# Decoder trunk with a mixture of experts: expert weights take the units of their ring in the order in which these are released

## The chip, the cores and the metric

The kernel runs on one core of a Trainium2 chip. The metric is the device time of one execution in microseconds (us). The kernel before took 1750.72 us, the median of three runs (1747.68, 1750.72 and 1752.5).

## What is computed

A trunk of two layers over 512 tokens of width 1024, all in float32. Layer 0 mixes tokens by RWKV-7 and by sparse attention, layer 1 by stick-breaking attention. Each layer then has a mixture of experts, which is all that the change touches:

```python
# hierarchical_moe: top-1 of 4 groups, then top-2 of its 8 experts; 32 experts in all
expert_idx, gates = ...                    # two experts for each of the 512 tokens
def expert_block(args):                    # w1, w3: 1024 x 512, w2: 512 x 1024
    xb, e = args
    return (jax.nn.silu(xb @ w1[e]) * (xb @ w3[e])) @ w2[e]
y = jnp.sum(y_asg.reshape(n_tok, 2, d) * gates[..., None], axis=1)
x = x + y
```

After both layers comes a final RMSNorm.

## The kernel before

A layer's end has two stages, each closed by a barrier of all engines. `router` does the mixer's output projection, chooses the experts and scatters the tokens' rows, sorted by expert, to the DRAM tensor `sorted_rows`: POOL issues two indirect DMAs for each of four tiles of 128 tokens (L581). `experts` then goes through the 32 experts, 48 rows each.

**Weights.** Each expert has three pieces (part 0 is w1, part 1 is w3, part 2 is w2) of 2 MiB each, 16 KB on each of 128 partitions. They are read from HBM once, into a ring of 11 units in SBUF. Piece p (expert p // 3, part p % 3) lies in unit p % 11 (`place`), so it may be loaded only once piece p - 11 has been used. SP issues all these loads (L634, and L641 for halves) and the loads of rows (L1055), in one written order, and waits in that same order.

The first eight units are loaded at the start of `router`. Units 8 and 9 (`GUEST`) first hold the output projection's weights. Once this is done, SP issues unit 8, then waits for the scatter of the rows, loads the rows of experts 0 to 2 from `sorted_rows` into three slots (`SLOTS`), and issues unit 9. Unit 10 is loaded at the start of `experts`. From there, for each expert n from 3, SP waits until the rows of expert n - 3 have been transposed, loads the rows of expert n, and then each part of expert n after the wait of `freed`: on `up_done` if the unit held w1 or w3, on `down_done` if it held w2. The last two experts (`HALVED`) come in halves, so that the first half of a product can start on the first half of the weights.

**TensorE's order in `experts`.** `turn_rows` transposes an expert's rows (L714), `gain_rows` on DVE copies them out with a gain (L783). `up` multiplies them by w1 and w3 (L726, L727; the two products lie side by side in the array, in eight steps over k); ACT takes the silu of one (L839), DVE multiplies it by the other (`hidden`, L791). `up` of expert n waits for `xT_out` (the rows of n) and for `hid_done` (the `hidden` of n - 1, which frees the PSUM bank). `turn_hidden` transposes the result (L748), `down` multiplies by w2 (L756), and `spread` (L778) puts the rows back on the tokens, added by DVE (L823). Below expert 19 (`OWN`) TensorE does `up` of n, `turn_hidden` of n - 1 and `down` of n - 1; from there on it does `up`, `turn_hidden` and `down` of the same expert.

At the layer's end the units of `GUEST` take what comes next: three tiles of the second layer's q/k/v weights (`LoadedAhead`, L1213) or the final norm's gain (`GainAhead`, L1228).

Of the kernel before, what the change touches and what calls it, by code (L numbers as in the profile page):

```python
# [31 lines left out]
KD = D // P  # L32
# [5 lines left out]
N_EXP = 32  # L38
# [13 lines left out]
class Core:  # L52


    def __init__(self, nc, ctx):
        self.nc, self.ctx, self.made, self.of_stage = nc, ctx, 0, []
# [118 lines left out]
class Arriving(InPlace):  # L175
# [6 lines left out]
    def load(self, sp):  # L182
        for t in range(TT):
            sp.dma_start(self.x[:, t, :], self.x_dram[t * P:(t + 1) * P, :]).then_inc(self.x_in[t], 16)
# [107 lines left out]
def router(nc, c, ctx, ps, x, xn, yT, gain_dram, w_group, w_expert, xrows, r, wts):  # L292
# [8 lines left out]
    LAST = TT - 1  # L301
    tok = lambda i: slice(order[i] * P, (order[i] + 1) * P)
    wr = c.sb("w_router", [P, KD, NL], ctx=ctx)
    g = r.gain
# [46 lines left out]
    with nc.Block() as block:  # L351

        @block.sync
        def _(sp):
            sp.dma_start(g[:, :], gain_dram.rearrange("(p k) -> p k", k=KD)).then_inc(gain_in, 16)
            sp.dma_start(wr[:, :, 0:N_GRP], w_group.rearrange("(p k) n -> p k n", k=KD)).then_inc(w_in, 16)
            for i in range(N_GRP):
                lo = N_GRP + i * EPG
                sp.dma_start(wr[:, :, lo:lo + EPG],
                             w_expert[i].rearrange("(p k) n -> p k n", k=KD)).then_inc(w_in, 16)  # L360
            wts.load(sp, range(GUEST[0]))
            sp.wait_ge(out_done, 2 * TT)
            wts.load(sp, GUEST[:1])
            for j in range(2):
                sp.wait_ge(scattered[j], 16 * TT)
            for n in range(SLOTS):
                r.load_rows(sp, xrows, n, n * CAP)
            wts.load(sp, GUEST[1:])

        @block.tensor  # L370
        def _(pe):
# [216 lines left out]
SLOTS = 3  # L588
XG = MB * D // (P * P)
UNIT, UNITS = KD * FF, 11  # L590
PARTS = (KD, KD, KF)
GUEST = (8, 9)
EXTRA = (0, 1, 2)


def place(n, part):

    use, j = divmod(len(PARTS) * n + part, UNITS)
    return j, use


HALVED = (N_EXP - 2, N_EXP - 1)
LOADS = [sum(place(n, part)[0] == j for n in range(N_EXP) for part in range(len(PARTS))) for j in range(UNITS)]


class ExpertWeights:
# [4 lines left out]
    def __init__(self, c):  # L611
        self.c = c
        self.landed = [c.lasting_sem(f"unit_in{j}") for j in range(UNITS)]
        self.rest_landed = [[c.lasting_sem(f"rest_in{n}_{part}") for part in range(2)] for n in HALVED]

    def start_layer(self, w1, w3, w2):
        self.dram, self.unit = (w1, w3, w2), {}
# [19 lines left out]
    def load_half(self, eng, n, part, half):  # L637

        k = PARTS[part] // 2
        rows = slice(half * k, (half + 1) * k)  # L640
        eng.dma_start(self.view(n, part)[:, rows, :], expert(self.dram[part], n, 2 * k)[:, rows, :]).then_inc(  # L641
            self.rest_landed[HALVED.index(n)][part] if half else self.landed[place(n, part)[0]], 16)

    def arrived(self, pe, n, part):

        j, use = place(n, part)
        pe.wait_ge(self.landed[j], 16 * (use + 1))

    def load_guest(self, eng, w_dram):

# [8 lines left out]

    def end_layer(self, c):  # L660

        c.of_stage += self.landed + [s for pair in self.rest_landed for s in pair]
        self.__init__(c)


def expert(w, e, k):

    return w[bass.ds(e, 1)].rearrange("o (p k) n -> p (o k) n", k=k)
# [3 lines left out]
def experts(nc, c, ctx, ps, x, xrows, r, gain_dram, wts, ahead):  # L672
# [8 lines left out]
    x_rows, g, row_of, slot_row, slot0, rows_in = r.x_rows, r.gain, r.row_of, r.slot_row, r.slot0, r.rows_in  # L681
# [11 lines left out]
    half = (slice(0, MB), slice(UP, UP + MB))  # L693
    GROUPS = 2 * TT

    xT_done, xT_out = c.sem("xT_done"), c.sem("xT_out")
    up_done, silu_done, hid_done = c.sem("up_done"), c.sem("silu_done"), c.sem("hid_done")
    hidT_done, hidT_out = c.sem("hidT_done"), c.sem("hidT_out")
    down_done, high_out, low_out = c.sem("down_done"), c.sem("y_high_out"), c.sem("y_low_out")
    compared, sel_made, spread_out, added = c.sem("compared"), c.sem("sel_made"), c.sem("y_spread"), c.sem("x_added")  # L700
    far_out, own = c.sem("further_slot_out"), c.sem("dve_own")

    LAST, OWN = N_EXP - 1, 19
    XSLOT, XUSES = N_EXP % SLOTS, N_EXP // SLOTS
    slot = lambda n: n % SLOTS
    use = lambda n: n // SLOTS
# [3 lines left out]
    def turn_rows(pe, j, u):  # L710
        pe.wait_ge(rows_in[j], 16 * u + 16)
        nc.tensor.ldweights(c.half[:, :], tile_position=(0, 0))
        for i in range(XG):
            last = nc.tensor.transpose(ps_x[:, i:XG * P:XG], x_rows[j][:, i, :], c.ident[:, :])  # L714
        last.then_inc(xT_done, 1)

    def up(pe, n, b, w1, w3, first_half, second_half):
        pe.wait_ge(xT_out, n + 1)
        if not isinstance(n, int) or n >= 1:
            pe.wait_ge(hid_done, n)  # L720
        for k in range(KD):
            if k == 0:
                first_half()
            if k == KD // 2:
                second_half()
            nc.tensor.matmul(ps_1[0:MB, :], xT[b][:, k, :], w1[:, k, :], start=k == 0, stop=k == KD - 1)  # L726
            last = nc.tensor.matmul(ps_3[UP:UP + MB, :], xT[b][:, k, :], w3[:, k, :],  # L727
                                    start=k == 0, stop=k == KD - 1)
        last.then_inc(up_done, 1)

    def up_expert(pe, n, before):
        def first_half():
            for part in range(2):
                wts.arrived(pe, n, part)

        def second_half():
            if n in HALVED:
                for part in range(2):
                    pe.wait_ge(wts.rest_landed[HALVED.index(n)][part], 16)

        up(pe, n, n % 2, wts.view(n, 0), wts.view(n, 1), first_half, second_half)
        spread(pe, before, range(TT // 2))
# [119 lines left out]
    with nc.Block() as block:  # L862

        @block.sync
        def _(sp):
            wts.load(sp, range(GUEST[-1] + 1, UNITS))

            def freed(n, part):

                gone, was = divmod(len(PARTS) * n + part - UNITS, len(PARTS))  # L870
                sp.wait_ge(down_done if was == 2 else up_done, gone + 1)

            for n in range(SLOTS, N_EXP):
                sp.wait_ge(xT_done, n - SLOTS + 1)
                r.load_rows(sp, xrows, slot(n), n * CAP)
                if n in HALVED:
                    for part in (0, 1):
                        freed(n, part)
                    for half_ in range(2):
                        for part in (0, 1):  # L880
                            wts.load_half(sp, n, part, half_)
                    freed(n, 2)
                    wts.load(sp, [len(PARTS) * n + 2])
                else:
                    for part in range(len(PARTS)):
                        if len(PARTS) * n + part >= UNITS:
                            freed(n, part)
                            wts.load(sp, [len(PARTS) * n + part])
            if ahead is not None:
                users = [max(n for n in range(N_EXP) for part in range(len(PARTS)) if place(n, part)[0] == j) for j in GUEST]  # L890
                sp.wait_ge(down_done, max(users) + 1)
                ahead.load(sp, [wts.unit[j] for j in GUEST])

            def more(e, b, m):
                end = sp.value_load(r.x_end[0:1, bass.ds(e, 1)], min_val=MB, max_val=N_ROWS)
                row = nc.s_assert_within(sp.snap(end - b * MB), 0, N_ROWS - MB, skip_runtime_bounds_check_because="further blocks lie inside the expert's rows")
                sp.wait_ge(down_done, m + N_EXP)
                r.load_rows(sp, xrows, XSLOT, row)
                for part in range(len(PARTS)):
                    wts.load_whole(sp, e, part, EXTRA[part])  # L900

            further(sp, more)

        @block.tensor
        def _(pe):
            turn_rows(pe, 0, 0)
            up_expert(pe, 0, -1)
            turn_rows(pe, 1, 0)
            for n in range(1, OWN):
                up_expert(pe, n, n - 2)  # L910
                turn_hidden(pe, n - 1)
# [15 lines left out]
            def more(e, b, m):  # L927
                n, u = m + N_EXP, m + XUSES

                def landed(part):  # L930
                    pe.wait_ge(wts.landed[EXTRA[part]], 16 * m + 16 * (LOADS[EXTRA[part]] + 1))

# [261 lines left out]
def odd_columns(g):  # L1194

    lo = (g * GC + 2 * D) % (3 * D)
    return slice(lo, lo + GC)


class LoadedAhead:  # L1200
# [5 lines left out]
        self.c, self.w = c, w_dram.rearrange("(p k) n -> p k n", k=KD)  # L1206
        self.raw_in = [c.lasting_sem(f"w_raw_in{i}") for i in range(self.N)]

    def load(self, sp, guest):
        halves = [tile[:, h * KD * GC:(h + 1) * KD * GC] for tile in guest for h in range(2)]  # L1210
        self.raw = [halves[i].rearrange("p (k n) -> p k n", k=KD) for i in range(self.N)]
        for g in range(self.N):
            sp.dma_start(self.raw[g], self.w[:, :, odd_columns(g)]).then_inc(self.raw_in[g], 16)  # L1213

    def raw_tiles(self):
# [4 lines left out]
class GainAhead:  # L1220
# [2 lines left out]
    def __init__(self, c, gain):  # L1223
        self.c, self.gain, self.gain_in = c, gain, c.lasting_sem("final_gain_in")

    def load(self, sp, guest):
        self.tile = guest[0][:, 0:D]
        sp.dma_start(self.tile, self.gain.rearrange("(o d) -> o d", o=1).to_broadcast([P, D])).then_inc(self.gain_in, 16)  # L1228


# [1719 lines left out]
```

## Time and profile before

| | |
|---|---|
| median of three runs | 1750.72 us (1747.68 to 1752.5) |
| the profiled execution | 1754.57 us |
| its span, first to last instruction | 1752.8 us |
| TensorE (PE) busy | 1637.4 us, 93% |
| VectorE (DVE) busy | 990.7 us, 57% |
| ScalarE (ACT) busy | 457.2 us, 26% |
| read from HBM | 454.67 MB |
| mean granted TensorE clock | 0.977 |

The two `experts` stages lie at about 484 to 955 us and 1270 to 1740 us, over half of the span. Times in rows are from the span's start. In a row of the timeline, the idle time of the engine before the instruction stands in brackets, with what seems to have ended it. An issue of a DMA on SP ("SPq") is only the issue; the transfer goes on beside it.

### The profile page before, as it was taken

The numbers are of one execution on the slowest core, as the hardware profiler recorded it, in microseconds if no ns is written. First come the engines' busy times: TensorE is split into PE (matmuls) and PEld (weight loads), VectorE is DVE, ScalarE is ACT, GpSimd is POOL, SyncE is SP. The second block draws the span as 40 slices with busy tenths as digits, with TensorE's granted clock in tenths as the row PEclk, the third lists the DMA queues.
The fourth block names the chain that finished last, engine by engine and source line by source line (L and its number), as shares of the span: only waits on it lengthen the run. The fifth ranks groups of instructions, "written<-read, shape, count | busy, mean of one in ns | idle before, by whom it ended". The sixth has DMA issues, their size and how long they took to land. (4 is left out here: it accounts for less than half of the span.)

```text
span 1752.8 us, 27282 instructions
## 1 busy us (share of the span) xinstructions
PE 1637.4 (93%) x11006; PEld 873.3 (50%) x11135; DVE 990.7 (57%) x1723; ACT 457.2 (26%) x773; POOL 156.8 (9%) x188
## 2 busy tenths in 40 slices
PE   8999877889889999999998999999899999999996
PEld 6756666655533333333334977665533333333333
DVE  4548676582436666666666322462536666666666
ACT  4363444372211111111112321462211111111112
POOL 2002424310100000000000040120100000000000
PEclk9999999899899999999999999999999999999999
DMA  6441000028589999999995250208589999999993
GB/s 199 115 126 55 7 3 4 11 89 321 219 350 425 425 426 426 426 428 425 426 423 219 76 192 25 96 1 346 214 362 428 426 426 425 426 427 427 426 422 153
DMA packets 100175, 475.35 MB, mean 271 GB/s; under 512 B 26833, under 2 KB 65745, under 8 KB 74448
## 3 DMA queue, kind: packets, MB, share of 16 engines
q1 hardware_dynamic: 96672, 460.99, 65.2%
q0 software_dynamic: 3376, 12.58, 1.9%
q8 instruction: 90, 1.47, 0.3%
q14 instruction: 37, 0.30, 0.1%
HBM read 454.67 MB, written 18.87 MB: 270 GB/s over the span
## 5 line engine op out<-in xcount | busy, mean ns | idle before, releaser
L726 PE MATMUL ps<-w_unit,xT 128*48 128x512 f32 x1024 | 455.5, 598 | 4.6 <-DVE xT L783 4.6
L727 PE MATMUL ps<-w_unit,xT 128*48 128x512 f32 x1024 | 455.6, 598 | 0.0
L823 DVE SCALAR_TENSOR_TENSOR x<-ps,gate_by_expert,x 128x512 f32<-128x512 f32 x512 | 348.4, 744 | 179.7 <-PE ps L778 179.6
L726 PEld LDWEIGHTS ps<-w_unit,xT 128*48 128x48 f32 x1024 | 126.7, 124 | 313.0 <-issue 307.3
L756 PE MATMUL ps<-w_unit,hidT 128*48 128x512 f32 x1024 | 247.7, 604 | 12.1 <-issue 12.1
L778 PE MATMUL ps<-y_high_low,slots_to_tokens 128*128 128x512 f32 x512 | 155.0, 424 | 8.0 <-DVE y_high_low L798 5.2
L846 ACT ACTIVATE y_high_low<-ps 48x512 fp32r<-48x512 f32 x128 | 75.8, 592 | 323.6 <-PE ps L756 322.0
L778 PEld LDWEIGHTS ps<-y_high_low,slots_to_tokens 128*128 128x128 f32 x512 | 86.5, 189 | 122.3 <-DVE x L823 55.9
L1297 PE MATMUL ps<-hT_high,w_high 128*128 128x512 f32 (+1 forms) x336 | 135.6, 404 | 6.4 <-PE ps L1299 4.1
L839 ACT ACTIVATE gate_act_hid<-ps 48x512 f32<-48x512 f32 x64 | 38.0, 593 | 373.1 <-PE ps L727 373.1
L1299 PE MATMUL ps<-hT_high,w_low 128*128 128x512 f32 (+1 forms) x336 | 132.8, 395 | 0.0
L1298 PE MATMUL ps<-hT_low,w_high 128*128 128x512 f32 (+1 forms) x336 | 132.3, 394 | 0.0
L727 PEld LDWEIGHTS ps<-w_unit,xT 128*48 128x48 f32 x1024 | 126.7, 124 | 0.0
L756 PEld LDWEIGHTS ps<-w_unit,hidT 128*48 128x48 f32 x1024 | 60.3, 123 | 120.7 <-issue 120.7
L791 DVE TENSOR_TENSOR gate_act_hid<-gate_act_hid,ps 48x512 f32<-48x512 f32 x64 | 44.3, 691 | 126.7 <-ACT gate_act_hid L839 109.7
L380 PE MATMUL ps<-w_unit,yT 128*128 128x512 f32 x256 | 113.8, 596 | 1.7 <-PEq L78 1.7
L798 DVE TENSOR_TENSOR y_high_low<-ps,y_high_low 48x512 fp32r<-48x512 f32 x128 | 88.1, 688 | 25.8 <-ACT y_high_low L846 22.8
L1297 PEld LDWEIGHTS ps<-hT_high,w_high 128*128 128x128 f32 (+1 forms) x336 | 63.3, 188 | 32.6 <-issue 17.3
L380 PEld LDWEIGHTS ps<-w_unit,yT 128*128 128x128 f32 x256 | 47.3, 190 | 54.6 <-issue 54.6
L1299 PEld LDWEIGHTS ps<-hT_high,w_low 128*128 128x128 f32 (+1 forms) x336 | 63.1, 188 | 15.1
L1298 PEld LDWEIGHTS ps<-hT_low,w_high 128*128 128x128 f32 (+1 forms) x336 | 63.3, 188 | 14.5 <-issue 0.2
L1534 DVE TENSOR_TENSOR_SCAN tail<-keep,zero 128x512 f32<-128x512 f32 (+3 forms) x64 | 49.3, 812 | 23.3 <-POOL keep L1521 23.3
(373 smaller groups left out, 1957.2 us busy)
## 6 DMA issues: line engine op xcount, KB each, us to landing
w_unit<-in_moe_w SPq DMA_DIRECT2D x184, 2048.0 KB, 28.3
w_unit<-in_moe_w SPq DMA_DIRECT2D x16, 1024.0 KB, 31.5
x_rows<-sorted_rows SPq DMA_DIRECT2D x64, 192.0 KB, 26.7
w_unit<-in_od_w_qkv SPq DMA_DIRECT2D x12, 1024.0 KB, 5.4
w_raw<-in_ev_w_in SPq DMA_DIRECT2D x10, 1024.0 KB, 6.2
sorted_rows<-bias SPq DMA_DIRECT2D x32, 192.0 KB, 5.6
w_unit<-in_ev_w_out SPq DMA_DIRECT2D x2, 2048.0 KB, 10.7
w_unit<-in_od_w_out SPq DMA_DIRECT2D x2, 2048.0 KB, 10.9
```

What stands on the lines that cost most here:

```text
L380: last = nc.tensor.matmul(ps_out[2 * (i % 2) + h][:, :], yT[:, f, tok(i)], w[h][:, f, :], start=f == 0, stop=f == KD - 1)
L726: nc.tensor.matmul(ps_1[0:MB, :], xT[b][:, k, :], w1[:, k, :], start=k == 0, stop=k == KD - 1)
L727: last = nc.tensor.matmul(ps_3[UP:UP + MB, :], xT[b][:, k, :], w3[:, k, :], start=k == 0, stop=k == KD - 1)
L756: last = nc.tensor.matmul(ps_y[h][half[h], :], hidT[:, k, :], w2[:, k, h * FF:(h + 1) * FF], start=k == 0, stop=k == KF - 1)
L778: nc.tensor.matmul(ps_c[t % 2 * 2 + h][:, :], sel_of(n)[:, t * P:(t + 1) * P], y[:, h, :], start=True, stop=True).then_inc(spread_out, 1)
L798: nc.vector.tensor_tensor(y[half[1 - h], h, :], ps_y[h][half[h], :], y[half[h], h, :].bitcast(F32), ALU.subtract).then_inc(low_out, 1)
L823: nc.vector.scalar_tensor_tensor(out=xs, in0=ps_c[i % 4][:, :], scalar=gate(t), in1=xs, op0=ALU.mult, op1=ALU.add).then_inc(added, 1)
L846: nc.scalar.activation(y[half[h], h, :], ps_y[h][half[h], :], ACT.Copy).then_inc(high_out, 1)
L1297: nc.tensor.matmul(out, lhsT[0], rhs[0], start=start, stop=False)
L1298: nc.tensor.matmul(out, lhsT[0], rhs[1], start=False, stop=False)
L1299: return nc.tensor.matmul(out, lhsT[1], rhs[0], start=False, stop=stop)
L1534: nc.vector.tensor_tensor_scan(tail[i % DEEP][:, a, 0:L][:, ::-1], keep[i % DEEP][:, a, 0:L][:, ::-1], zero[:, 0:L], 1.0, ALU.mult, ALU.ad ...
```

## The change

The ring's order is no longer p % 11. `in_order_of_release` writes down in which order the pieces are used up (where `down` of n - 1 follows `up` of n, that is (n, 0), (n, 1), (n - 1, 2)), and piece p takes the unit that is the (p - 11)th to be released. SP waits for that piece. The first four pieces that are loaded again (w2 of expert 3, all of expert 4) come in halves: their first halves wait for the first four of the eight steps of `up` of expert 0 and 1 (`up_half`), their second halves for `up_done`. `turn_rows` of expert 1 moves from behind `up` of expert 0 to the middle of it. Units 8 and 9 are both loaded before the wait for the scatter. At the layer's end, SP waits for each guest unit by itself; with the new order the last user of unit 9 is w2 of expert 31, and that of unit 8 is w2 of expert 28, as before.

```diff
             sp.wait_ge(out_done, 2 * TT)
-            wts.load(sp, GUEST[:1])
+            wts.load(sp, GUEST)
             for j in range(2):
                 sp.wait_ge(scattered[j], 16 * TT)
             for n in range(SLOTS):
                 r.load_rows(sp, xrows, n, n * CAP)
-            wts.load(sp, GUEST[1:])
...
+def in_order_of_release():
+
+    pieces = [(0, 0), (0, 1)]
+    for n in range(1, OWN):
+        pieces += [(n, 0), (n, 1), (n - 1, 2)]
+    pieces += [(OWN - 1, 2)]
+    for n in range(OWN, N_EXP):
+        pieces += [(n, 0), (n, 1), (n, 2)]
+    return pieces
+
+
+def places():
+
+    released, where, uses = in_order_of_release(), {}, [0] * UNITS
+    for p in range(N_EXP * len(PARTS)):
+        j = p if p < UNITS else where[released[p - UNITS]][0]
+        where[divmod(p, len(PARTS))] = j, uses[j]
+        uses[j] += 1
+    return released, where, uses
...
+EARLY = [divmod(p, len(PARTS)) for p in range(UNITS, UNITS + 4)]
+IN_HALVES = EARLY + [(n, part) for n in HALVED for part in range(2)]
...
+            if isinstance(n, int) and n < len(EARLY) // 2 and k == KD // 2 - 1:
+                last.then_inc(up_half, 1)
...
+            if n == 0:
+                turn_rows(pe, 1, 0)
...
-                gone, was = divmod(len(PARTS) * n + part - UNITS, len(PARTS))
+                gone, was = RELEASED[len(PARTS) * n + part - UNITS]
                 sp.wait_ge(down_done if was == 2 else up_done, gone + 1)
+
+            def load_early(gone):
+                for half_, done in enumerate((up_half, up_done)):
+                    sp.wait_ge(done, gone + 1)
+                    for piece in EARLY[2 * gone:2 * gone + 2]:
+                        wts.load_half(sp, *piece, half_)
...
-                if n in HALVED:
+                if n - SLOTS < 2:
+                    load_early(n - SLOTS)
+                elif n in HALVED:
...
             up_expert(pe, 0, -1)
-            turn_rows(pe, 1, 0)
             for n in range(1, OWN):
...
-                sp.wait_ge(down_done, max(users) + 1)
-                ahead.load(sp, [wts.unit[j] for j in GUEST])
+                ahead.load(sp, [wts.unit[j] for j in GUEST], lambda i: sp.wait_ge(down_done, users[i] + 1))
```

## Rows read from the trace of the kernel before

**Rows 1.** Windows: busy time of each engine, granted clock, DMA share, GB/s
```profile
485.00:490.00 5.00, 4.43 (x12) 1.21 (x14) 0.52 (x1) 0.18 (x1) 0.00 (x0) 0.50 0.99 398
495.00:512.00 17.00, 15.54 (x76) 6.07 (x77) 4.89 (x8) 2.70 (x5) 0.00 (x0) 1.00 0.75 285
600.00:700.00 100.00, 100.00 (x452) 38.89 (x467) 64.42 (x101) 15.45 (x30) 0.00 (x0) 1.00 1.01 426
```
**Rows 2.** Waits of TensorE, 485 to 960 us: total us, times, longest
```profile
PE ps L756 <- issue: 6.1, 13, 0.5
PE ps L778 <- DVE y_high_low L798: 2.6, 1, 2.6
PE ps L726 <- DVE xT L783: 2.5, 2, 1.4
```
**Rows 3.** Timeline of SP at 705 us and of TensorE at 733 us
```profile
705.28 0.33 SPq L634 DMA_DIRECT2D w_unit<-in_moe_w  x1
...
733.05 0.59 PE L726 MATMUL ps<-w_unit,xT 128*48 128x512 f32 x1
```
**Rows 4.** Line L634 at 705.2 to 705.5 us, its last row
```profile
DMA to landing us min/median/max: 26.7/26.7/26.7
```
**Rows 5.** Timeline, all engines, 494 to 498 us
```profile
495.57 0.55 PE L714 MATMUL ps<-ident,x_rows 128*128 128x128 f32 x3
495.65 0.33 SPq L634 DMA_DIRECT2D w_unit<-in_moe_w  x1
495.65 0.59 ACT L839 ACTIVATE gate_act_hid<-ps 48x512 f32<-48x512 f32 x1 [10.47 <-PE ps L727]
...
496.16 0.56 DVE L783 TENSOR_TENSOR xT<-ps,moe_gain 128x384 f32<-128x384 f32 x1 [10.64 <-PE ps L714]
...
496.75 0.69 DVE L791 TENSOR_TENSOR gate_act_hid<-gate_act_hid,ps 48x512 f32<-48x512 f32 x1
...
497.54 0.60 PE L726 MATMUL ps<-w_unit,xT 128*48 128x512 f32 x1 [1.42 <-DVE xT L783]
```
**Rows 6.** Timeline of TensorE around a later `turn_rows`
```profile
518.02 0.55 PE L714 MATMUL ps<-ident,x_rows 128*128 128x128 f32 x3
518.52 1.92 PE L756 MATMUL ps<-w_unit,hidT 128*48 128x512 f32 x8
```
**Rows 7.** Timeline of SP at the ends of the two `router` stages
```profile
463.63 0.33 SPq L634 DMA_DIRECT2D w_unit<-in_moe_w  x1
...
479.59 1.28 SPq L1055 DMA_DIRECT2D x_rows<-sorted_rows  x3
...
1265.96 1.28 SPq L1055 DMA_DIRECT2D x_rows<-sorted_rows  x3
```
**Rows 8.** Line L581, scatters of tiles 2 (465 us) and 3 (474 us)
```profile
DMA to landing us min/median/max: 7.9/8.5/9.0
...
DMA to landing us min/median/max: 3.4/3.6/3.7
```
**Rows 9.** Windows as in rows 1, last scatters of the first `router`
```profile
471.00:474.00 3.00, 2.38 (x17) 2.38 (x18) 1.83 (x10) 0.31 (x2) 0.00 (x0) 0.50 0.83 337
474.00:476.00 2.00, 2.00 (x17) 1.91 (x16) 1.72 (x7) 0.00 (x0) 1.38 (x1) 0.50 0.12 47
476.00:480.00 4.00, 4.00 (x32) 2.31 (x31) 2.00 (x4) 0.00 (x0) 0.96 (x1) 0.76 0.64 262
```
**Rows 10.** Timeline of DVE: its last instruction in each `router`
```profile
482.41 0.29 DVE L564 TENSOR_TENSOR gate_by_expert<-gated 128x128 f32<-128x128 f32 x1
...
1268.08 0.29 DVE L564 TENSOR_TENSOR gate_by_expert<-gated 128x128 f32<-128x128 f32 x1
```
**Rows 11.** Timeline of TensorE: its first instruction in each `experts`
```profile
483.95 0.55 PE L714 MATMUL ps<-ident,x_rows 128*128 128x128 f32 x3 [3.10 <-PEq L78]
...
1269.78 0.90 PE L714 MATMUL ps<-ident,x_rows 128*128 128x128 f32 x3 [3.25 <-PEq L78]
```
**Rows 12.** Line L1055, the three loads of rows at 479.6 us
```profile
DMA to landing us min/median/max: 2.5/2.7/4.0
```
**Rows 13.** Timeline: TensorE's last `down` of layer 0, ACT's third weight tile after it
```profile
944.92 1.92 PE L756 MATMUL ps<-w_unit,hidT 128*48 128x512 f32 x8
...
978.59 1.91 ACT L1267 ACTIVATE w_high<-w_unit 128x2048 fp32r<-128x2048 f32 x1
```
**Rows 14.** DMA issues, on the page: count, KB each, median us to landing
```profile
w_unit<-in_od_w_qkv SPq DMA_DIRECT2D x12, 1024.0 KB, 5.4
```

More of the change, by code:

```diff
@@ L593 @@
 EXTRA = (0, 1, 2)
+LAST, OWN = N_EXP - 1, 19
+def in_order_of_release():
[13 more added lines that the diff above has]
+    return released, where, uses
+RELEASED, PLACES, LOADS = places()
 def place(n, part):
-    use, j = divmod(len(PARTS) * n + part, UNITS)
-    return j, use
+    return PLACES[n, part]
 HALVED = (N_EXP - 2, N_EXP - 1)
-LOADS = [sum(place(n, part)[0] == j for n in range(N_EXP) for part in range(len(PARTS))) for j in range(UNITS)]
+EARLY = [divmod(p, len(PARTS)) for p in range(UNITS, UNITS + 4)]
+IN_HALVES = EARLY + [(n, part) for n in HALVED for part in range(2)]
 class ExpertWeights:
@@ L613, in __init__ @@
         self.landed = [c.lasting_sem(f"unit_in{j}") for j in range(UNITS)]
-        self.rest_landed = [[c.lasting_sem(f"rest_in{n}_{part}") for part in range(2)] for n in HALVED]
+        self.rest_landed = {piece: c.lasting_sem(f"rest_in{piece[0]}_{piece[1]}") for piece in IN_HALVES}
     def start_layer(self, w1, w3, w2):
@@ L641, in load_half @@
         eng.dma_start(self.view(n, part)[:, rows, :], expert(self.dram[part], n, 2 * k)[:, rows, :]).then_inc(
-            self.rest_landed[HALVED.index(n)][part] if half else self.landed[place(n, part)[0]], 16)
+            self.rest_landed[n, part] if half else self.landed[place(n, part)[0]], 16)
     def arrived(self, pe, n, part):
@@ L647, in arrived @@
         pe.wait_ge(self.landed[j], 16 * (use + 1))
+        if (n, part) in EARLY:
+            pe.wait_ge(self.rest_landed[n, part], 16)
     def load_guest(self, eng, w_dram):
@@ L660, in end_layer @@
     def end_layer(self, c):
-        c.of_stage += self.landed + [s for pair in self.rest_landed for s in pair]
+        c.of_stage += self.landed + list(self.rest_landed.values())
         self.__init__(c)
@@ L696, in experts @@
     xT_done, xT_out = c.sem("xT_done"), c.sem("xT_out")
+    up_half = c.sem("up_half")
     up_done, silu_done, hid_done = c.sem("up_done"), c.sem("silu_done"), c.sem("hid_done")
@@ L701, in experts @@
     far_out, own = c.sem("further_slot_out"), c.sem("dve_own")
-    LAST, OWN = N_EXP - 1, 19
     XSLOT, XUSES = N_EXP % SLOTS, N_EXP // SLOTS
@@ L738, in second_half @@
                 for part in range(2):
-                    pe.wait_ge(wts.rest_landed[HALVED.index(n)][part], 16)
+                    pe.wait_ge(wts.rest_landed[n, part], 16)
+            if n == 0:
+                turn_rows(pe, 1, 0)
         up(pe, n, n % 2, wts.view(n, 0), wts.view(n, 1), first_half, second_half)
@@ L1207, in __init__, with load @@
         self.raw_in = [c.lasting_sem(f"w_raw_in{i}") for i in range(self.N)]
-    def load(self, sp, guest):
+    def load(self, sp, guest, free):
         halves = [tile[:, h * KD * GC:(h + 1) * KD * GC] for tile in guest for h in range(2)]
@@ L1212, in load @@
         for g in range(self.N):
+            if g % 2 == 0:
+                free(g // 2)
             sp.dma_start(self.raw[g], self.w[:, :, odd_columns(g)]).then_inc(self.raw_in[g], 16)
@@ L1224, in __init__, with load @@
         self.c, self.gain, self.gain_in = c, gain, c.lasting_sem("final_gain_in")
-    def load(self, sp, guest):
+    def load(self, sp, guest, free):
         self.tile = guest[0][:, 0:D]
+        free(0)
         sp.dma_start(self.tile, self.gain.rearrange("(o d) -> o d", o=1).to_broadcast([P, D])).then_inc(self.gain_in, 16)
```

## The prediction

> **What bounds the kernel now.** I first read the windows in steps of 100 us. In the middle of both `experts` stages they show two things near full at once: TensorE is busy 100.00 of 100.00 us, and the DMA engines have a share of 1.01 and move 426 GB/s [rows 1]. So the question is which of the two the other waits for. The view of TensorE's waits over the first `experts` stage answers it: the idle times are 6.1 us before `down` in the late experts, 2.6 us behind DVE at the change of order, 2.5 us behind `gain_rows`, and some smaller ones, and none of them is put down to a load of weights [rows 2]. TensorE sets the pace; the weights only just keep up. How closely, I worked out from SP's issues, their time to landing and TensorE's first use of each piece, for all 96 pieces of both layers. The tightest is w3 of expert 18: issued at 705.28, landed 26.7 us later at 731.98, used at 733.05 [rows 3, 4], 1.1 us to spare. A stream that is always in time costs nothing, however full it is, and a faster one wins nothing.
>
> **The ring's order and the early halves.** They let loads start earlier. Around 495 to 512 us the DMA share is 0.75 [rows 1], so about 17 x 0.25 = 4.3 us of transfer time is free there; unit 9, issued 16 us earlier, brings another 2.097 MB / 426 GB/s = 4.9 us. As the DMA engines are full from then on, all later pieces should land some 9 us earlier, and the tightest margin should grow from 1 to about 10 us. TensorE didn't wait for any of them, so the gain in time is 0. What it adds is off the path too: four more DMA issues on SP in each layer, one more wait for each early piece (a passed wait shows no idle time in rows 2; I take 0, at most 0.1 us), five more semaphores. What it may lose: rows of later experts queue behind these loads, but in the same order as before and behind loads that land earlier. At the end, the third q/k/v tile now waits for w2 of expert 31. Its `down` ends at 946.8, the load takes 5.4 us when nothing is ahead of it [rows 13, 14], so it lands at about 953 and is read at 978.6: 25 us to spare, cost 0. Without that cover it would cost the 5.4 us.
>
> **The second turn of rows.** Before, TensorE ends `up` of expert 0, turns the rows of expert 1 (495.57, 0.55 us), and stands idle 1.42 us until 497.54. The profile puts this down to `gain_rows` [rows 5]. If so, moving the turn ahead would remove the turn's visible end and the wait. But `up` of expert 1 waits for two things. `gain_rows` ends at 496.16 + 0.56 = 496.72; `hidden` of expert 0 ends at 496.75 + 0.69 = 497.44, and TensorE starts 0.10 us after this one, 0.8 us after the other [rows 5]. The wait that ends last is `hidden`, and its chain is `up` of 0, silu (495.65, 0.59 us), `hidden` (0.69 us). The change takes the 0.5 us by which DVE was late (496.24 to 496.75, as `gain_rows` was on it) out of this chain, less some 0.1 us of hand-over. But it puts the turn inside `up` of expert 0, ahead of the silu: 0.50 us from its start to the next matmul [rows 6], up to 0.6 us with the switch. Sum per layer: +0.55 - 0.40 = +0.15 us. Bounds: -1.4 us if the label in rows 5 is right, +0.6 us if nothing comes back. I take +0.15, since the end of `hidden` is the row nearest to the start. For two layers, +0.3 us.
>
> **Unit 9 ahead of the scatter.** This is the one edit that can reach the path by more. Unit 9 is now issued right behind unit 8 (463.63), while the scatters of tiles 2 and 3 go to DRAM; before it came behind them and behind the rows. A scatter that runs beside unit 8's load lands in 8.5 us, one that runs alone in 3.6 us [rows 8]. The DMA engines still have room: from 471 to the issue of the rows at 479.59 [rows 7] the idle share is 3 x 0.17 + 2 x 0.88 + 3.6 x 0.36 = 3.6 us [rows 9], of which some 0.4 us is the last landing's latency. Unit 9 needs 4.9 us. If the engines waste nothing, the last scatter ends 4.9 - 3.2 = 1.7 us later. Upper bound: it waits for all of unit 9, 4.9 us. Lower bound: 0.
>
> What this does to the start of `experts`: the barrier waits for SP and DVE. In layer 0 SP would issue the rows at 481.3 and be done 1.28 us later, at 482.6; DVE ends at 482.41 + 0.29 = 482.70 [rows 10], so the barrier doesn't move. The first rows land 2.5 us behind their issue [rows 12], at 483.8, and TensorE's first turn was at 483.95 [rows 11]: cost 0. In layer 1 SP has less room: 1265.96 + 1.7 + 1.28 = 1268.9 against DVE's 1268.08 + 0.29 = 1268.4, and the barrier moves by 0.6 us. With the upper bound the rows would land at 487.0 and 1273.4, 3.0 and 3.6 us later than TensorE's first turns. I take 0 and 0.6 us.
>
> The Trainium skill bears on which end is right: its page "DMA: Bandwidth & Descriptors" (section "Queues, rings and completion order") says that each DMA engine takes turns between the queues that have work for it, packet by packet. By that rule the scatter, on POOL's queue, isn't held back for the whole of unit 9 on SP's queue, which speaks for the small end of the range; rows 8 alone don't decide it, as the slow scatter there ends about when unit 8 does.
>
> **Sum.** 0 (ring) + 0.3 (turn) + 0 + 0.6 (start of `experts`) = +0.9 us. The profiled execution took 1754.57 us (span 1752.8 us and 1.8 us around it), so it would become 1755.5 us; it is 3.9 us above the median of the runs, and nothing in the sum depends on that. From the median of 1750.72 us I get 1751.6 us.
>
> **Rivals.**
> - *The scatter starves.* The last scatter waits for all of unit 9, the rows come late, and TensorE starts both stages late: +3.0 + 3.6 + 0.3 = +6.9 us, 1757.6 us. For it: the 8.5 us in rows 8. Against it: the idle share in rows 9, enough for most of unit 9 before the last scatter's packets come. It decides from the point where the last scatter lands over 1.7 us later in layer 0, or over 1.1 us in layer 1, and reaches the measurable only above about 4 us in both.
> - *The label is right.* The wait before the second `up` was `gain_rows` and goes: 2 x -1.4 + 0.6 = -2.2 us, 1748.5 us. For it: the label in rows 5. Against it: the 0.10 us between the end of `hidden` and the start.
> - *The clock.* TensorE runs the first half of each `experts` stage's first `up` at a granted 0.50 of its clock, that is 1.2 instead of 2.4 GHz, after it stood idle for 3.1 us [rows 1, 11]. The moved start may shorten or lengthen such a stretch. In the 5 us of rows 1 half the work is lost, 2.5 us, so each layer may go up or down by about that: 1746 to 1757 us.
> - *The change doesn't do what it says.* SP might be held by an earlier wait, and the 0.75 in rows 1 stays. Then the margins stay at 1 us and the time is the forecast's, 1751.6 us. Only if the new order delays a piece by more than its margin does TensorE wait. Each piece waits for the same or an earlier release, so I see no such piece.
>
> **How the numbers follow.** Three runs of the kernel before lie 4.8 us apart; a change under 0.3% (5.3 us) can't be told from none. Chances: forecast 0.72 (with the ring that does nothing), label 0.10, starved scatter 0.10, clock 0.08. The forecast, the label and most of the clock's cases are within 0.3%; the starved scatter is above it. The range of 1747.5 to 1757 takes in the label's case, nearly all of the clock's, and most of the way to the starved scatter. Faster 0.05, same 0.85, slower 0.10.
>
> **What would show it.** Right: TensorE's waits look as in rows 2, with no load of weights among them; the margin of w3 of expert 18 is 8 to 13 us; the DMA share around 495 to 512 us is above 0.85; the second `up` starts 0.1 us behind `hidden`, and the first has a turn in its middle; the rows' issue moves from 479.59 to about 481.3 and in layer 1 by as much. Wrong: the first turn of a stage comes over 2 us after its barrier would allow, or the second `up` starts right behind the first, or the kernel is over 5 us faster, which would mean that loads did hold up TensorE where the profile shows no wait.

## The result, and the profile after

The changed kernel takes 1756.81 us (median of 20 runs, 1748.92 to 1762.36) against 1752.64 us of the kernel before (20 runs): ratio 1.0021, 95% interval 1.0011 to 1.0030. That is 3.7 us more (1.9 to 5.3), 2.8 us above the forecast's +0.9 us. The median lies inside the forecast range, 0.2 us below its upper end of 1757; 1.9 us of the way there are no effect of the change, as the kernel before has a median of 1752.64 us over 20 runs and not the 1750.72 us of three. The profiled execution took 1756.1 us, with a span of 1754.4 us and a mean granted clock of 0.981.

The waits of TensorE over the first `experts` stage (who waited, for whom; total us, times, longest) are nearly those of [rows 2]. The third row belongs to the next stage; the fourth is the wait before the second `up`, which is no longer put down to `gain_rows`. Again no load of weights is among them:

```profile
PE ps L788 <- issue: 6.1, 13, 0.5
PE ps L810 <- DVE y_high_low L830: 2.6, 1, 2.6
PE ps L112 <- PEq L78: 1.6, 1, 1.6
PE ps L754 <- issue: 1.5, 1, 1.5
```

The loads did get ahead. The DMA share early in the stage, 0.75 in [rows 1] and 0.72 from 493 to 510 us, is now 1.00 (columns as in [rows 1]):

```profile
493.00:510.00 17.00, 15.50 (x75) 5.78 (x75) 3.92 (x7) 2.70 (x5) 0.00 (x0) 1.00 1.00 404
```

and w3 of expert 18, which was issued at 705.28 and had 1.1 us to spare [rows 3, 4], is issued eight microseconds earlier (first the timeline of SP, then line L660's time to landing, then the timeline of TensorE at its first use). It lands at 723.7 and has 8.5 us to spare:

```profile
697.38 0.80 SPq L660 DMA_DIRECT2D w_unit<-in_moe_w  x2
```
```profile
DMA to landing us min/median/max: 26.3/26.3/26.3
```
```profile
732.26 0.59 PE L754 MATMUL ps<-w_unit,xT 128*48 128x512 f32 x1
```

What got worse is the end of `router`. The timeline of SP shows units 8 and 9 going out together, and the rows 19.25 and 19.98 us behind them; before, the rows came 15.96 us behind unit 8 in layer 0 [rows 7]:

```profile
461.55 0.80 SPq L660 DMA_DIRECT2D w_unit<-in_moe_w  x2
...
480.80 0.34 SPq L1093 DMA_DIRECT2D x_rows<-sorted_rows  x1
...
1250.48 0.81 SPq L660 DMA_DIRECT2D w_unit<-in_moe_w  x2
...
1270.46 0.80 SPq L1093 DMA_DIRECT2D x_rows<-sorted_rows  x2
```

Line L580, the last two scatters of each layer: 6.9 and 7.0 us to landing, where [rows 8] have 3.6:

```profile
DMA to landing us min/median/max: 6.8/6.9/7.0
...
DMA to landing us min/median/max: 6.8/7.0/7.2
```

TensorE's first turns in the timeline now follow an idle time of 4.4 and 5.4 us, not 3.1 and 3.25 [rows 11]:

```profile
483.26 0.90 PE L742 MATMUL ps<-ident,x_rows 128*128 128x128 f32 x3 [4.44 <-PEq L78]
...
1273.06 0.90 PE L742 MATMUL ps<-ident,x_rows 128*128 128x128 f32 x3 [5.36 <-PEq L78]
```

From the issue of unit 8 to the first turn it took 20.3 us (463.63 to 483.95) and 19.8 us before, and takes 21.7 and 22.6 us now: 1.4 and 2.8 us more. Two traces alone would be thin evidence, as this distance varies without the edit too. Over the six kernels of this document that load all of unit 9 behind the rows it is 19.0 to 20.6 us in layer 0 and 19.8 to 20.5 us in layer 1; over the three that load all of it early, 21.7 us and 22.4 to 22.6 us. The averages differ by 2.1 and 2.3 us, 4.4 us in all, where the one pair gives 4.2.

### The profile page after: what moved, and what is told of

It is laid out like the page before. It is cut to its first block and busy times, and to the rows that moved or that the text cites. A ratio compares the mean times of both kernels' runs of the same rounds, so it can differ in the third digit from the quotient of the medians.

```text
span 1754.4 us, 27294 instructions
## 1 busy us (share of the span) xinstructions
PE 1631.9 (93%) x11006; PEld 871.2 (50%) x11135; DVE 991.7 (57%) x1723; ACT 457.3 (26%) x773; POOL 155.5 (9%) x188
```

## The experiments: which edit costs the time

**Unit 9 behind the rows again**, all else as changed.

```diff
-            wts.load(sp, GUEST)
+            wts.load(sp, GUEST[:1])
...
                 r.load_rows(sp, xrows, n, n * CAP)
+            wts.load(sp, GUEST[1:])
```

> The changed kernel with one edit undone: unit 9 is issued behind the scatter and the rows again; the ring, the early halves and the moved turn stay. Theory (unit 9's traffic beside the last scatter delays the rows): the last scatter lands some 3.5 us behind its issue instead of 6.8 and 7.2, TensorE's first turn comes 1.2 to 1.5 us behind DVE's last instruction of the stage in both layers (changed kernel: 2.6 and 3.5), and the time is that of the kernel before within 1 us, some 3 us under the changed kernel. Rival (the ring's order or the moved turn costs the time): the time stays 3 to 4 us above the kernel before. The margin of w3 of expert 18 should be some 5 us, between 1.1 (before) and 8.5 (changed).

Measured: 1751.73 us against 1751.88 of the kernel before, ratio 0.9999 (0.9986 to 1.0012). The loss is gone. The last scatters land in 3.5 and 3.6 us (line L581 in this kernel), the first turn comes 1.3 and 1.4 us behind DVE's last instruction of `router`, as it did before, and 20.6 and 20.5 us behind the issue of unit 8:

```profile
DMA to landing us min/median/max: 3.4/3.5/3.7
...
DMA to landing us min/median/max: 3.4/3.6/3.7
```

The margin of w3 of expert 18 is 6.6 and 5.0 us (1.0 and 1.3 before, where the 1.1 of the rows is rounded; 8.5 and 7.4 in the changed kernel).

**Unit 9 early, alone**: the kernel before with that edit only.

> The kernel before with one edit of the change alone: unit 9 is issued right behind unit 8. Theory: the last scatter lands 6.8 to 7.2 us behind its issue, TensorE's first turn comes 2.4 to 3.6 us behind DVE's last instruction, and the kernel is 2 to 4 us slower than the one before. Rival (the other parts cost the time): the last scatter still lands in 3.5 us and the time is that of the kernel before. The margin of w3 of expert 18 grows from 1.1 to at most 6 us.

Measured: 1755.61 us, ratio 1.0028 (1.0016 to 1.0039), 4.9 us slower. The last scatters land in 6.9 and 7.2 us, the first turn comes 4.0 and 4.1 us behind DVE, 21.7 and 22.4 us behind unit 8's issue. The ratio's interval is 2.8 to 6.8 us, so it takes in most of the 2 to 4 us expected. Added to the kernel before, the edit gives the slowdown; taken out of the changed kernel, it takes it away. How much of the 4.9 us is the late start alone is less clear: the granted clock was 0.979 on average over these 11 runs and 0.981 over the 29 of the kernel before. The edit gives nothing back: the margin of w3 of expert 18 is 0.9 us in both layers, where up to 6 us had been expected. This fits a stream that, with the old ring, waits for releases and not for the DMA engines.

**Unit 9 in halves**, the first half early, the second behind the rows.

```diff
-            wts.load(sp, GUEST)
+            wts.load(sp, GUEST[:1])
+            wts.load_half(sp, 3, 0, 0)
...
                 r.load_rows(sp, xrows, n, n * CAP)
+            wts.load_half(sp, 3, 0, 1)
...
-IN_HALVES = EARLY + [(n, part) for n in HALVED for part in range(2)]
+IN_HALVES = [(3, 0)] + EARLY + [(n, part) for n in HALVED for part in range(2)]
...
-        if (n, part) in EARLY:
+        if (n, part) in EARLY + [(3, 0)]:
```

> The changed kernel with unit 9 in halves: the first half (1 MiB) is issued behind unit 8, the second behind the rows. Theory A (the engines do the same total of work, and only what doesn't fit into the 3.2 us that were idle comes on top): 2.5 us of load fit, the last scatter lands within 1 us of its 3.5 us, and the first turn comes 1.2 to 1.8 us behind DVE. Theory B (turns by packet, 4 KB of the scatter for each larger packet of weights, slow the scatter however little there is): the last scatter still takes 5 us or more behind its issue. The time lies 1 to 3 us under the changed kernel by A, within 1 us of it by B.

Measured: 1753.16 us, ratio 1.0003 (0.9993 to 1.0013). The last scatters take 4.4 and 4.0 us, the first turn comes 1.6 and 1.4 us behind DVE. Theory A holds: half a unit nearly fits into what was idle, a whole one doesn't. The margins are 7.2 and 7.0 us.

**The turn behind the first up product**, all else as changed.

```diff
-            if n == 0:
-                turn_rows(pe, 1, 0)
...
             up_expert(pe, 0, -1)
+            turn_rows(pe, 1, 0)
```

> The changed kernel with the turn of expert 1's rows back behind the first up product. Theory (the wait that ends last before the second up is hidden, so the move is worth nothing): from the start of the first up to the start of the second it takes within 0.3 us of the changed kernel, once the share of the stretch at half clock is taken out, and the time is the same within noise. Rival (the wait was for the rows of expert 1): the second up starts 1.4 us later in each layer, 2.8 us more in all.

Measured: 1757.49 us, 6 runs, ratio 1.0039 (1.0025 to 1.0053). Taken alone, the runs speak for the rival rather than the theory: the ratio is 3 us above the changed kernel's, and the rival's price was 2.8. But the intervals overlap, and the granted clock over these six runs was 0.978 on average against 0.980 in the changed kernel. The traces decide. In the timeline of the changed kernel the turn sits inside the product, whose steps are else 0.43 us apart, and stretches one of them from 490.30 to 491.35, by 0.62 us:

```profile
490.30 0.59 PE L754 MATMUL ps<-w_unit,xT 128*48 128x512 f32 x1
...
490.87 0.55 PE L742 MATMUL ps<-ident,x_rows 128*128 128x128 f32 x3
491.35 0.63 PE L754 MATMUL ps<-w_unit,xT 128*48 128x512 f32 x1
...
495.04 0.59 ACT L871 ACTIVATE gate_act_hid<-ps 48x512 f32<-48x512 f32 x1 [10.55 <-PE ps L755]
495.66 0.69 DVE L823 TENSOR_TENSOR gate_act_hid<-gate_act_hid,ps 48x512 f32<-48x512 f32 x1 [3.65 <-ACT gate_act_hid L871]
...
496.45 0.60 PE L754 MATMUL ps<-w_unit,xT 128*48 128x512 f32 x1 [1.46 <-issue]
```

From the silu to the second `up` it takes 1.41 us, 1.89 before (495.65 to 497.54, [rows 5]), and TensorE still idles 1.46 us, 0.10 us behind the end of `hidden` at 496.35, although `gain_rows` is long done. From the first `up` to the second, with half of the time at half clock taken out, it takes 8.97 or 8.98 us with the turn behind the product (this kernel and the one before, both layers) and 9.15 or 9.16 us with the turn inside: the move costs 0.19 us a layer, and the rival's 1.4 us is not there.

## What the new ring is worth

The margin of w3 of expert 18 rises by 5.6 and 3.8 us even without the early unit 9. TensorE's two orders take 13.99 us (below `OWN`) and 14.52 us (from it on) for an expert; its loads, 6.49 MB at the 426 GB/s of [rows 1], take 15.2 us. So spare time of the loads can be traded for experts in the faster order. Three kernels move only `OWN` besides: two have the ring's order and the early halves, with unit 9 and the turn where they were before; one is the kernel before.

```diff
-LAST, OWN = N_EXP - 1, 19
+LAST, OWN = N_EXP - 1, 23
```

**The ring, `OWN` at 23.**

> The changed kernel with unit 9 behind the rows and the turn behind the first up product again (so the ring's order and the early halves stay), and TensorE changes its order at expert 23 instead of 19. Theory (the ring bought spare time for the loads, 5.0 and 6.6 us at w3 of expert 18, and each further expert in the first order takes 13.99 instead of 14.52 us and uses up 15.2 - 13.99 = 1.2 us of it): no load holds TensorE up, the tightest margin is 0 to 2 us, and the kernel takes 2 x 4 x 0.53 = 4.2 us less than the one before, less 0.6 us for the early waits: -3.6 us. Rival (the spare time is not real or the second order was what kept the layer's end supplied): TensorE waits before up 22 or in the last experts, and the time is that of the kernel before or above it.

Measured: 1743.3 us against 1751.89, ratio 0.9959 (0.9942 to 0.9975), 7.2 us faster. No load is waited for, the tightest margins are 1.0 and 0.7 us as forecast. The gain is twice the sum, and the sum lies outside the interval. In its profile the change of order, 24.9 us from `up` of expert 18 to the next one before, takes 23.6 us at the new place, with no stretch at half clock in either layer. That is 2.6 us of the missing 3.6 in this one trace; the same place at half clock in other kernels shows the longer time. The granted clock of every run is on record, and it points the same way. It was 0.9832 on average over these 12 runs and 0.9805 over the 34 of the kernel before. Among those 34, the 8 with a clock of 0.979 or less took 1754.8 us on average and the 10 with 0.982 or more 1749.4 us (mean clocks 0.9781 and 0.9824), 1.3 us for each 0.001. By this estimate the higher clock is worth some 3.4 us, about all that the sum lacks. Why this kernel is granted more is not shown.

**The ring, `OWN` at 27.**

> As with expert 23, but the order changes at expert 27. Theory: 8 x 1.2 = 9.9 us are used up and 5.0 to 6.6 us are there, so TensorE stands idle before up of experts 23 to 26 for 3 to 5 us in each layer in all, against 4.2 us gained in each: the time lies within 2 us of the kernel before, and above that with the order changed at 23. Rival (the loads are not the limit): no idle time, 8.5 us less than before.

Measured: 1754.18 us, ratio 1.0012 (0.9999 to 1.0025). The waits of TensorE in the first `experts` stage now have a load at the top, within the 3 to 5 us expected; in the second stage it is 2.9 us in three waits, just under. The gain is used up:

```profile
PE ps L755 <- DMA w_unit<-in_moe_w: 4.8, 4, 1.8
```

**The kernel before, `OWN` at 23.**

> The kernel before with only the expert at which the order changes moved from 19 to 23. Theory (the new ring is what makes this possible): the margin of 1.0 us is used up, TensorE waits for w3 of experts 19 to 22 for some 4 us in each layer, against 2.1 us gained: 2 to 4 us slower than before. Rival (the ring is not needed for it): 4.2 us faster.

Measured: 1756.93 us, ratio 1.0029 (1.0017 to 1.0041), slower by 5.1 us, a little more than expected. Same view:

```profile
PE ps L756 <- issue: 4.2, 9, 0.5
PE ps L726 <- DMA w_unit<-in_moe_w: 4.0, 4, 1.1
```

So experts 19 to 22 come 15.2 us apart, at the pace of the loads. The same `OWN` gains 7.2 us with the new ring and the early halves and loses 5.1 with the old ring: the spare time is real.

**Half of unit 9 early, `OWN` at 24.**

> The ring's order, the early halves, the turn behind the first up product, unit 9 in halves (the first behind unit 8, the second behind the rows), and the order changed at expert 24. Theory: the margin at expert 18 is about 7 us and 5 x 1.2 = 6.2 us are used up, so there is no wait or one under 1 us; 2 x 5 x 0.53 = 5.3 us gained, 0.6 us for the early waits and 0.5 us for the scatter beside half a unit lost: -4 us against the kernel before. Rival: the half costs as much at the start as it brings at the end, and the time is that with expert 23 or above it.

Measured: 1744.21 us against 1751.89, ratio 0.9955 (0.9941 to 0.9968), 7.9 us faster than before, the best median ratio of all; no load is waited for, with margins of 0.7 and 0.2 us. It can't be told from the kernel with `OWN` at 23 and unit 9 late. Here both layers have a stretch at half clock at the change of order, so the clock at that place doesn't explain why this one, too, gains more than its 4 us. Over all of its runs, though, the granted clock was 0.9825 on average, which is worth some 2.5 us by the estimate above.

**The same at 23.**

> As with half of unit 9 ahead and the order changed at expert 24, but at expert 23. Theory: the margin stays above 1 us, no load is waited for, and the time is 1 us above that with expert 24 and 0.5 to 1 us above that with expert 23 and unit 9 behind the rows; all three lie 6 to 9 us under the kernel before. Rival (the margin of 0.2 to 0.7 us at expert 24 is sometimes missed in runs without the profiler): the time is at or under that with expert 24.

Measured: 1745.6 us against 1750.58, ratio 0.9966 (0.9955 to 0.9978), 6.0 us faster, with a mean granted clock of 0.9829. The rival fails: the thin margin at `OWN` 24 costs nothing that the runs show.

**No early halves, `OWN` at 23.**

```diff
-EARLY = [divmod(p, len(PARTS)) for p in range(UNITS, UNITS + 4)]
+EARLY = []
...
-                if n - SLOTS < 2:
-                    load_early(n - SLOTS)
-                elif n in HALVED:
+                if n in HALVED:
```

> The kernel with the ring's order, unit 9 and the turn where they were, and the order changed at expert 23, but without the early halves: the first four reloads come whole, behind up_done or down_done. Theory (the 0.15 us that the changed kernel loses in each of the intervals of experts 4 and 5 are the second waits of the early pieces): from the second up to up of expert 18 it takes 235.51 us as before, not 235.82. The halves brought the first reload forward by some 4 us, so the margins shrink by 1 to 4 us, the tightest was 0.7 to 1.0, and TensorE may wait for w3 of expert 22, up to 3 us in each layer; time between that with the halves and 4 us above it. Rival (the 0.30 us come from the new places of the pieces, and the halves bring no margin): 235.82 us stays, and the time is the same within 0.5 us.

Measured: 1749.72 us against 1750.58, ratio 1.0002 (0.9988 to 1.0016). From the second `up` to that of expert 18 it takes 235.51 us again, against 235.8 in every kernel with the halves. The place is `down` of experts 3 and 4. In the timeline, the changed kernel first, its matmuls come 0.65 us behind the start of the turn ahead of them; without the second wait 0.50 us, as in [rows 6]. What the second wait waits for had long been there (the last of the second halves landed at 514.6 us). That the wait is the cause is inferred from the place, as no run has the halves without it:

```profile
544.90 0.55 PE L742 MATMUL ps<-ident,x_rows 128*128 128x128 f32 x3
545.55 1.03 PE L788 MATMUL ps<-w_unit,hidT 128*48 128x512 f32 x3
```
```profile
542.00 0.55 PE L743 MATMUL ps<-ident,x_rows 128*128 128x128 f32 x3
542.50 1.06 PE L787 MATMUL ps<-w_unit,hidT 128*48 128x512 f32 x4
```

The halves are worth their 0.6 us all the same. Without them the margin of w3 of expert 18 is 3.1 and 3.7 us, against 5.8 and 7.0 with them, and TensorE then waits for loads, 2.7 us in layer 0 (the row) and 1.0 us in layer 1:

```profile
PE ps L755 <- DMA w_unit<-in_moe_w: 2.7, 3, 1.0
```

The time is 6.3 to 7.5 us above that with the halves (ratio 1.0002 against 0.9966 and 0.9959), outside what was expected. The waits less the 0.6 us make 3.1 us of it. The granted clock was 0.9809 on average and 0.9829 and 0.9832 with the halves, some 2.5 to 3 us by the same estimate, so little is left beyond the intervals. Why the clock differs is again not shown.

## Why the prediction was right, point by point

The account of what bounds the kernel held. One term of the sum was far too small, and the range held it by little.

- **TensorE sets the pace; faster loads win nothing**: right. No wait for a load in the kernel before or after, and the kernel with the ring but without the early unit 9 runs at 0.9999.
- **The margin grows by 9 us**: 7.5 and 6.2 us measured, less than forecast (the margin in layer 1 is 7.4 us, under the 8 to 13), and the split was wrong. I gave unit 9 4.9 us of it. Alone it brings nothing, on top of the ring about 2 us. The kernels with `OWN` at 23 split the rest: some 2 us for the ring's order alone, some 3 us for the halves.
- **A passed wait costs at most 0.1 us**: wrong. A second wait before `down` costs 0.15 us, twice in each layer, and these 0.6 us in all were put at nothing in the sum. The one ahead of `up` costs nothing that the trace shows.
- **The second turn of rows, +0.15 us a layer**: 0.19 us. The label in [rows 5] named `gain_rows`; the wait that ended last was `hidden`.
- **Unit 9 ahead of the scatter**: the mechanism was right (what doesn't fit beside the scatter comes on top) and the size was far off. This is the term that failed: I had the last scatter 1.7 us late "if the engines waste nothing", and it is 3.4 us late in layer 0 (issue to landing of the last one 3.42 before, 6.83 now) and 3.7 us in layer 1. The start of `experts` then moves by 1.4 and 2.8 us and not by 0 and 0.6: 4.2 us where the sum had 0.6. The windows of the changed kernel (columns as in [rows 9]) show how long the engines stay full:

```profile
468.00:475.00 7.00, 5.57 (x32) 4.62 (x33) 4.25 (x20) 0.31 (x2) 2.34 (x2) 0.59 0.99 375
475.00:479.00 4.00, 3.82 (x43) 2.71 (x41) 2.89 (x8) 0.00 (x0) 0.00 (x0) 0.87 0.97 394
479.00:481.00 2.00, 0.00 (x0) 0.00 (x0) 1.46 (x7) 0.00 (x0) 0.00 (x0) 1.00 0.09 37
```

The DMA view has the end of the scatter in finer steps. Its row gives the busy share of the engines in 40 slices, in tenths, first for the changed kernel from 475 to 481 us, then for the kernel before from 476 to 480 us:

```profile
DMA  6969989998999999999999999842211100000000
```
```profile
DMA  0006799899997997159999969789880000000000
```

The engines now stay full until 478.9, 5.0 us behind the last scatter's issue at 473.90; before, until 479.0, 2.9 us behind the issue at 476.10. These 2.1 us are the work that doesn't fit, which the sum had as 1.7. The rest the sum did not have at all. Before, the share falls from full to nothing at once; now it takes until 480.4, when the last packet ends, with 8 packets or fewer in flight from 479.0 on and one from 479.9 on. That is 1.4 us more, and the landing comes 0.3 to 0.4 us behind the last packet in both. In layer 1 the two parts are 1.8 and 2.1 us. Why the end is drawn out is not shown.
- **The starved scatter.** By the marks that the prediction itself set (a last scatter over 1.7 us later in layer 0, over 1.1 us in layer 1), this rival, and not the forecast, describes the start of the stages. Its 4.9 us for the landing and 6.9 us for the time were too much. The forecast's range took in most of the way to it, and the measured median ended near that end. That the range held in spite of a term that was 3.6 us too small is in part luck.
- **The sum from the traces** is 4.2 (start) + 0.4 (turn) + 0.6 (waits) = +5.2 us, at the upper end of the measured 1.9 to 5.3.
- **The clock** is not shown to give any of this back. In this pair of traces, 4.8 and 3.5 us between the first and the second `up` lie at half clock, 6.0 and 5.2 before, worth 1.5 us, which would bring 5.2 down to the measured 3.7. But it doesn't go with the late start. The kernel with unit 9 early alone starts as late and has 5.5 and 5.9 us; the kernel before with `OWN` at 23 starts as early as it did with 19 and has 4.7 and 5.2. And over its 20 runs the changed kernel has a mean granted clock of 0.9801, no higher than the 0.9810 and 0.9805 of the kernel before in the later comparisons. So the exact match would be a matter of which two executions were traced.

The share between the queues, which I had left open, can be read in the DMA view of the changed kernel from 469 to 474 us, while the scatter of tile 2 goes beside unit 9 (queue, kind: packets, MB, share of 16 engines):

```profile
q1 hardware_dynamic: 103, 1.62, 87.2%
q0 software_dynamic: 99, 0.40, 19.5%
```

Both queues got nearly the same number of packets, but a packet of the weights holds 16 KB and one of the scatter 4 KB. This agrees with the Trainium skill, "DMA: Bandwidth & Descriptors", section "Queues, rings and completion order", by which an engine takes turns packet by packet, if what the profile counts as a packet is what is meant there. The turns don't spare the scatter much when its packets are a quarter of the others' size. They also show whom the last scatter waits for. From 475 to 481 us the weights' queue moves only 20 packets and the scatter's 440 with 1.59 MB, more than the 1.05 MB of one tile's rows (128 tokens, twice, at 4 KB). So the last scatter, tile 3's, stands mostly behind tile 2's in its own queue, which unit 9 had held back.

## What to carry to other kernels

A stream that is always in time is not a bound, however full it is: make room in it only together with the edit that spends the room. Here that edit is more experts in the faster order; by the sum it turned 0 into some 4 us, and the runs show 6 to 8, of which the granted clock may be 2 to 3. Before a prefetch is moved ahead, look at who shares its DMA engines just then. If the shared transfer is what the next stage waits for, fill only the time that is idle. And where the profile names one of two waits, compare both ends with the start; the one that ends last is worth the edit. A sum from one pair of traces that meets the measured difference to a tenth needs the same check as one that doesn't: see whether each term is there in the other kernels too.

## What the runs showed of the hardware

- A transfer of 4 KB packets beside one of 16 KB packets gets a fifth of the bytes (0.40 of 2.02 MB) at a nearly equal count of packets, 99 and 103.
- When the last scatter ran alone, the engines went from full to idle within 0.1 us at its end; in the changed kernel it took 1.5 us (layer 0) and 2.2 us (layer 1), and the landing came 0.3 us behind the last packet.
- A second semaphore wait that had long been passed went with 0.15 us more before `down` and nothing before `up`; why is open.
